# Paged attention over a cache: key steps in pairs, transposes shared by two engines, scores by full-depth runs of 128 keys

## The reference

```python
def latent_scores(q_lat, q_pe, c, k_pe):
    s = jnp.einsum('bqhc,bkc->bhqk', q_lat, c) + jnp.einsum('bqhr,bkr->bhqk', q_pe, k_pe)
    return s.astype(jnp.float32) * MLA_SCALE

def sample_attention(q_lat, q_pe, c_new, kpe_new, c_past, kpe_past):
    s_past = latent_scores(q_lat, q_pe, c_past, kpe_past)
    ...
    p = jax.nn.softmax(jnp.concatenate([s_past, s_new], axis=-1), axis=-1).astype(c_new.dtype)
    return jnp.einsum('bhqk,bkc->bqhc', p[..., :P], c_past) + jnp.einsum('bhqk,bkc->bqhc', p[..., P:], c_new)
```

## Time and profile before

| | |
|---|---|
| median of 3 runs | 1033.61 us (1033.48 to 1036.86) |
| the profiled execution's own time | 1032.82 us |
| its span in the trace | 1030.9 us |
| PE busy, DVE busy, ACT busy, POOL busy | 982.4, 506.8, 445.0, 157.9 us |
| the cache attention, first transpose to the last values product | 407.6 to 568.2 us |
| one of its steps, in the middle of the loop | 9.58 us |

### The profile page before, as it was taken

The page is one execution under the profiler, slowest core; times in us unless marked ns, Lnnn a source line. Parts: engine busy times, 40 slices in busy tenths (PEclk is TensorE's granted clock), DMA queues, the critical chain, the costliest instruction groups (busy, mean ns, idle before and its releaser), DMA issues.

```text
span 1030.9 us, 20604 instructions
## 1 busy us (share of the span) xinstructions
PE 982.4 (95%) x8588; PEld 846.4 (82%) x8588; DVE 506.8 (49%) x992; ACT 445.0 (43%) x963; POOL 157.9 (15%) x257
## 2 busy tenths in 40 slices
PE   4999999999989999899999899999999999999997
PEld 4988899877757556566665799999999999999996
DVE  5665867565475485354444532633343234334423
ACT  5545637566646676344444423431232134113312
POOL 1020500255511201344541000000000000000000
PEclk9999969999999999999999899999999999999999
DMA  7312111220024501577772321422222222222302
GB/s 247 122 46 83 43 42 42 62 48 11 2 68 113 208 1 37 195 238 267 237 241 90 109 83 41 144 82 83 87 102 99 82 83 82 83 86 98 105 1 88
DMA packets 31655, 102.58 MB, mean 100 GB/s; under 512 B 14023, under 2 KB 14967, under 8 KB 25218
## 3 DMA queue, kind: packets, MB, share of 16 engines
q1 hardware_dynamic: 22346, 63.50, 18.7%
q0 software_dynamic: 9216, 37.75, 10.7%
HBM read 96.45 MB, written 4.22 MB: 98 GB/s over the span
## 4 chain that ended last, share of the span: by engine, by line
PE 87%; DVE 6%; ACT 3%; issue 2%; DMA 1%; SPq 0%; DVEq 0%; ACTq 0%
PE PS L589 17%; PE PS L591 17%; PE PS L590 17%; PE PS L1078 7%; PE PS L1089 3%; PE PS L1113 3%; PE PS L724 2%; PE PS L1096 2%; PE PS L797 1%; PE PS L828 1%; PE PS L880 1%; PE PS L979 1%; PE PS L571 1%; DMA RAW<-in_w_stream 1%; PE PS L698 1%
## 5 line engine op out<-in xcount | busy, mean ns | idle before, releaser
L589 PE MATMUL PS<-XH,WH 128*128 128x272 f32 (+1 forms) x928 | 271.4, 292 | 1.8 <-DVE WL L1721 1.8
L591 PE MATMUL PS<-XH,WL 128*128 128x272 f32 (+1 forms) x928 | 270.3, 291 | 0.0
L590 PE MATMUL PS<-XL,WH 128*128 128x272 f32 (+1 forms) x928 | 269.5, 290 | 0.0
L589 PEld LDWEIGHTS PS<-XH,WH 128*128 128x128 f32 x928 | 175.9, 190 | 6.8 <-issue 4.2
L590 PEld LDWEIGHTS PS<-XL,WH 128*128 128x128 f32 x928 | 176.2, 190 | 0.0
L591 PEld LDWEIGHTS PS<-XH,WL 128*128 128x128 f32 x928 | 175.9, 190 | 0.0
L1222 ACT ACTIVATE WH<-RAW 128x2048 fp32r<-128x2048 f32 x46 | 88.0, 1913 | 203.1 <-PE PS L591 203.1
L589 PE MATMUL PS<-NH,WH 128*128 128x272 f32 x512 | 149.1, 291 | 0.8 <-DVE WL L1721 0.8
L591 PE MATMUL PS<-NH,WL 128*128 128x272 f32 x512 | 147.6, 288 | 0.0
L590 PE MATMUL PS<-NL,WH 128*128 128x272 f32 x512 | 146.6, 286 | 0.0
L1721 DVE TENSOR_TENSOR WL<-RAW,WH 128x2048 fp32r<-128x2048 f32 (+1 forms) x48 | 108.1, 2252 | 64.6 <-ACT WH L1222 64.2
(11 more groups left out here) (323 smaller groups left out, 1473.0 us busy)
## 6 DMA issues: line engine op xcount, KB each, us to landing
RAW<-in_w_stream SPq DMA_DIRECT2D x47, 1024.0 KB, 4.8
XN<-in_hin SPq DMA_DIRECT2D x4, 512.0 KB, 6.2
out_y_p<-YO SPq DMA_DIRECT2D x4, 512.0 KB, 2.7
CST<-in_big SPq DMA_DIRECT2D x1, 1132.5 KB, 12.8
SS<-in_sstate SPq DMA_DIRECT2D x1, 1024.0 KB, 5.1
out_ssm_s<-SS SPq DMA_DIRECT2D x4, 256.0 KB
CN<-in_cache,IDX POOLq DMA_INDIRECT x64
WQN<-in_wq SPq DMA_DIRECT2D x3, 256.0 KB, 5.8
```

The source lines that it names most:

```text
L589: pe.matmul(PS[:, b, 0:n], wh, xh[:, k, c:c + n], start=(k == 0), stop=False)
L590: pe.matmul(PS[:, b, 0:n], wh, xl[:, k, c:c + n], start=False, stop=False)
L591: last = pe.matmul(PS[:, b, 0:n], wl, xh[:, k, c:c + n], start=False, stop=(k == DT - 1))
```

## The change

The steps are taken in **pairs** `m` (steps `2m` and `2m + 1`).

- The first 128 latent columns of each key are transposed by PE as before (L1084 in the changed kernel), four units to a step, into two PSUM banks in turn (4 and 7), and ACT alone copies them (`cache_copy`, L1685). The copy also sorts the keys, so that the 128 keys of one quarter `q` of the partitions stand in a row.
- The other 128 latent columns and the 32 rotary ones, five blocks of 32, are transposed by DVE in blocks of 32x32 from `CN` to `CB` (`block_transpose`, L2213, one for each sequence and step, 640 numbers on each partition). Nothing goes through PSUM there, and POOL's packing is gone.
- Scores stand in PSUM banks 0 to 3, one bank for each quarter of the partitions, 256 keys of a pair in each. `column_scores(n)` makes 16 matmuls of 128 keys over 128 rows. `block_scores(m)` makes 80 matmuls of 256 keys, each on 32 rows and 32 columns of the array (`QS` holds the queries laid out anew for that, filled by 32 small DMAs on SP's queue ahead of the loop).
- One maximum over 1024 scores on each row, one correction and one accumulation to a pair; two exponentials, two transposes of P (banks 5 and 0), two copies, two values products.
- `gather(n)` still waits for `ce_pv` of step `n - 4`; an odd one waits for `column_scores(n - 2)` as well.

```diff
-    cn_at = [[x + rows_of * b for b in range(4)] for x in (w_at, w_at + 4 * rows_of, x_at + 4 * rows_of, r1)]
+    cn_at = [[x + rows_of * b for b in range(4)] for x in (w_at, w_at + 4 * rows_of, x_at + DT * T * 4, r1)]
...
+            sp.wait_ge(sem("dve_step"), DVE_STEP["q_padded"])
+            for q in range(4):
+                rows = slice(32 * q, 32 * q + 32)
+                for s in range(4):
+                    src = slice(32 * s, 32 * s + 32)
+                    sp.dma_start(QS[rows, :, s, :], QF[src, :, 1, :]).then_inc(sem("wkbt_in"), 16)
+                    sp.dma_start(QS[rows, :, 4, src], QRF[src, :, src]).then_inc(sem("wkbt_in"), 16)
...
+            def block_scores(m):
+
+                pe.wait_ge(sem("cb_done"), 8 * m + 8)
+                for x in range(5):
+                    for q in range(4):
+                        rows = slice(32 * q, 32 * q + 32)
+                        for b in range(4):
+                            heads = slice(32 * b, 32 * b + 32)
+                            last = pe.matmul(PS[heads, q, 0:2 * P], QS[rows, m // 4, x, heads],
+                                             CB[b][rows, x, :, :, :].rearrange("p s j k -> p (s j k)"),
+                                             start=False, stop=(x == 4))
                 last.then_inc(sem("ct_used"), 1)
...
+            def column_scores(n):
+
+                s = n % 2
+                pe.wait_ge(sem("ct_copied"), 4 * n + 4)
+                if s == 0 and n >= 2:
+                    pe.wait_ge(sem("ce_exp"), n)
+                    pe.wait_ge(sem("ce_ptc"), n)
+                for q in range(4):
+                    for b in range(4):
+                        heads = slice(32 * b, 32 * b + 32)
+                        last = pe.matmul(PS[heads, q, P * s:P * s + P], QF[:, n // 8, 0, heads],
+                                         CT[s][b][:, q, :, :].rearrange("p j k -> p (j k)"),
+                                         start=(s == 0), stop=False)
+                last.then_inc(sem("ct_used"), 1)
...
+            step_transposes(0)
+            step_transposes(1)
+            column_scores(0)
+            for m in range(8):
+                column_scores(2 * m + 1)
+                block_scores(m)
+                if m < 7:
+                    step_transposes(2 * m + 2)
+                cache_p(2 * m)
+                cache_p(2 * m + 1)
+                for x in range(8):
+                    cache_values(2 * m + x // 4, x % 4)
+                if m < 7:
+                    column_scores(2 * m + 2)
+                    step_transposes(2 * m + 3)
...
+            for x in range(8):
+                cache_copy(x // 4, x % 4)
+            for m in range(8):
+                if m < 7:
+                    cache_copy(2 * m + 2, 0)
+                    cache_copy(2 * m + 2, 1)
+                cache_exp(m)
+                cache_copy_p(2 * m)
+                correction(m)
+                cache_copy_p(2 * m + 1)
+                if m < 7:
+                    cache_copy(2 * m + 2, 2)
+                    cache_copy(2 * m + 2, 3)
+                    for b in range(4):
+                        cache_copy(2 * m + 3, b)
...
+            def block_transpose(n, b):
+                if b == 0:
+                    dve.wait_ge(sem(f"cn_in{n % 4}"), 64 * (n // 4 + 1))
+                    if n >= 2:
+                        dve.wait_ge(sem("ct_used"), 3 * (n // 2 - 1) + 3)
+                dve.transpose(CB[b][:, :, n % 2, :, :].rearrange("p x j k -> p j x k"),
+                              CN[n % 4][b][:, :, P:].rearrange("p j (x c) -> p j x c", c=32)).then_inc(sem("cb_done"), 1)
...
+            for x in range(8):
+                block_transpose(x // 4, x % 4)
+            for m in range(8):
+                cache_max(m)
+                if m < 7:
+                    for x in range(8):
+                        block_transpose(2 * m + 2 + x // 4, x % 4)
+                accumulate(m)
...
-            for n in range(2, 16):
-                if n >= 3 and n + 1 < 16:
-                    pool.wait_ge(sem("ce_pv"), n - 2)
-                    gather(n + 1)
-                pack_rope(n)
+            for n in range(4, 16):
+                pool.wait_ge(sem("ce_pv"), n - 3)
+                if n % 2:
+                    pool.wait_ge(sem("ct_used"), 3 * (n // 2 - 1) + 2)
+                gather(n)
```

More of the change, by code:

```diff
@@ L1075, in cache_transposes @@
                     pe.wait_ge(sem(f"cn_in{n % 4}"), 64 * (n // 4 + 1))
                 for j in range(4):
-                    src = CN[n % 4][u % 4][:, j, P * (u // 4):P * (u // 4) + P] if u < 8 else KRN[n % 2][:, j, :, :]
-                    last = pe.transpose(PS[:, CT_BANKS[x % 4], P * j:P * j + P], src, ident)
+                    last = pe.transpose(PS[:, 4 + 3 * (x % 2), P * j:P * j + P], CN[n % 4][b][:, j, 0:P], ident)
                 last.then_inc(sem("ct_mm"), 1)
-            def cache_scores(n, c):
-                if c == 0 and n >= 2:
-                    pe.wait_ge(sem("ce_exp"), n - 1)
-                g, bank = n // 8, 3 + n % 2
-                for b in range(4):
-                    wait_copied(pe, n, 4 * c + b)
-                for b in range(4):
-                    last = pe.matmul(PS[32 * b:32 * b + 32, bank, :], QF[:, g, c, 32 * b:32 * b + 32], CT[4 * c + b][:, :],
-                                     start=(c == 0), stop=False)
-                last.then_inc(sem("ct_used"), 1)
@@ L1117, in _, with cache_values @@
-            for n in range(18):
-                for u in range(9):
-                    if n < 16:
-                        cache_transposes(n, u)
-                    if 1 <= n <= 16 and u == 1:
-                        cache_scores(n - 1, 1)
-                        cache_rope_scores(n - 1)
-                    if n >= 2 and u == 3:
-                        cache_values(n - 2)
-                    if n < 16 and u == 5:
-                        cache_scores(n, 0)
-                    if 1 <= n <= 16 and u == 8:
-                        cache_p(n - 1)
+            def cache_values(n, j):
+                s = n % 2
+                if j == 0:
+                    pe.wait_ge(sem("ce_ptc"), n + 1)
+                    if s == 0 and n >= 2:
+                        pe.wait_ge(sem("acc_done"), n // 2)
+                for b in range(4):
+                    last = pe.matmul(PS[32 * b:32 * b + 32, 6, 0:KV], PTE[:, 4 * s + j, 32 * b:32 * b + 32],
+                                     CN[n % 4][b][:, j, 0:KV], start=(s == 0 and j == 0), stop=(s == 1 and j == 3))
+                if j == 3:
+                    last.then_inc(sem("ce_pv"), 1)
```

189 lines of the change are left out of this document (82 added, 107 removed).

## The result

The changed kernel takes **1081.33 us** (median of 4 runs, 1077.98 to 1083.93) against 1033.78 for the kernel before (4 runs): a ratio of 1.0453, interval 1.0431 to 1.0475. It is slower by 4.5%, where 1009 us and a gain were forecast. The profiled execution took 1083.93 us, 1082.1 of it in the trace.

The account below looks back on a forecast made before the run. PE was taken to bound the kernel (busy 95%), then the gathers at 16.6 us a pair: 27.7 us less, 3 back for the clock, so 24.7 off 1032.8 gives 1008.1, plus 0.8 for the median: 1009 us, range 995 to 1036.

Parts of the forecast that it names:

- the sum: Whole kernel: start to 418.0, six cycles of 16.6 us, then 23.0; 27.7 us less, 24.7 after a clock allowance.
- Rival 5: Loop: engines stand still while DMA engines are full; a 3.7 us stop every second pair gives 1024 us; chance 0.10.
- the 3 us that I had put aside for the clock: Allowance in the total for PE's clock falling once or twice in the loop: 3 us.
- Rival 2: Loop: PE's clock falls to its lower level in every pair, some 3 us a pair, giving 1027 us; chance 0.14.
- forecast 15.3: Loop: the cycle of a pair that the engines alone give, without waiting for gathers, 15.3 us.
- The cycle of 16.6 that the gathers set: Loop: the even gather's keys land at x+16.5, so a pair takes 16.6 us and PE waits 1.3 (bounds 15.8 and 17.3).
- rival 3: Loop: DVE's block transposes are slow, 3.3 us each instead of 0.86, giving a cycle of 30 and 1105 us; chance 0.08.
- block_scores, 2.2 forecast: PE in each pair: 160 passes of 256 keys in ten turns, all 16 tiles at once, 2.2 us.
- rival 4: block_scores on PE: row groups follow one another, 8.6 us, giving 1052 us; chance 0.09 for the full case.
- The test I gave: Changed trace: the forecast is wrong if PE waits for `cb_done` or block_scores shows 4 us or more.

Follow-up runs that it names:

- Run 12: Changed kernel, but from step 4 on each of the four indirect DMAs of a step fetches 64 bytes per partition instead of 4608: 1082.72 us, ratio 1.0462.
- run 5: Changed kernel with the gathers of steps 4 to 15 replaced by plain DMAs of the same bytes from SP's queue, same waits: 1016.41 us.
- run 1: Changed kernel with the gathers of steps 4 to 15 left out (old keys used again): 1011.36 us.
- run 9: Changed kernel with the keys of steps 4 to 15 fetched by plain DMAs from POOL's own queue, same waits and bytes: 1016.08 us.
- run 2: Changed kernel with 64 of the 80 matmuls of block_scores left out: 1008.82 us.
- run 7: Changed kernel with only one of the four indirect DMAs of each step from 4 on, other keys old: 1019.34 us.
- run 3: Changed kernel without the odd gather's wait for column_scores: 1021.46 us.
- run 17: Changed kernel with the odd step's four indirect DMAs issued at separate points, the even step's four still in a row: 1024.72 us, ratio 0.9959.
- run 15: Changed kernel with the odd gather waiting for the end of block_scores instead of column_scores: 1043.7 us, ratio 1.0106.

## Why the prediction was wrong

**The step that failed** is the sum's price for PE's work beside a gather. It counts `block_scores`, the transposes and the column scores at the pace that they have alone, and lets a gather cost PE something only when it lands. Rival 5, "engines stand still while the DMA engines are full", had the matter, with the wrong cause and too low a price. The fact behind it was read rightly: DVE's stop of 3.70 us with its input done is the hold. But I laid it to the DMA share of 1.01 and to eight gathers in a row, and gave it one stop in every second pair, 4 x 3.7. Run 12 has the hold at a share of 0.03, and run 5 has none at 0.78; it comes with the issues of every gather, so twice in a pair.

What it measured, for a pair of 27.0 us against 15.8 in run 1, from stage start to stage start: block_scores 9.8 for 3.3 (+6.5); the odd step's transposes 5.4 for 3.2 and the column scores ahead of them 1.9 for 1.0 (+3.1); the even step's transposes and the odd step's column scores, at the lower clock, 3.2 for 2.5 and 1.9 for 1.0 (+1.6). That is 11.2. From the first to the last even step's transposes, 426.97 to 591.44, six pairs take 164.5 us where six of 16.6 were forecast: 64.9 more. The start has 9.0 more (427.0 for 418.0). Of these run 1 has 4.7 too, on a chip without the hold: `block_scores` begins at half clock there and takes 6.9 us for 2.2. The rest is the hold of the first column scores (6.4 us for 1.95). The end has 3.9 more. With the 3 us that I had put aside for the clock this gives 74.8 of the 75.8 between 1083.9 and 1008.1.

**Rival 2, the clock:** right in kind, too small alone. It falls in every pair, after PE has got its passes in fives and sixes. Of the 11.2 us the lower clock is 1.6 as above, about 1.7 in the last 79 passes of block_scores (3.33 us at half clock, an estimate: half at full), and up to 0.9 in its first 53 (2.0 us, where the pace of run 1 gives 1.1), some 4 in all; I had said 3. It is a consequence: without the hold it stays full in the pairs shown of runs 1, 5 and 9.

**Right:** where PE isn't held, its cycle is nearly as laid out: 15.8 us (forecast 15.3), in run 1 and in some pairs of runs 5 and 9. The cycle of 16.6 that the gathers set shows in run 2, where they do bind, at 17.3. A gather of the changed kernel takes 9.6 to 10.6 us from issue to last byte (10.2), the even one starts 2.23 us behind the values product (2.24). A block transpose is 0.81 us (0.86), so rival 3 falls, and the maximum 1.23 (1.2).

**Luck:** the 16.7 us of runs 5, 7 and 9 look like the forecast's 16.6 and aren't. No DMA stands in the chain of these pairs; a stop inside `block_scores` makes them longer than 15.8. In the changed kernel the keys are never waited for in the chain either, since PE comes later than they do.

**Without the hold,** 1009 us isn't shown either. The changed kernel itself never ran on such a chip. The nearest there are run 3 (1021.46, beside 1027.32) and run 17 (1024.72, beside 1028.87): gains of 0.6 and 0.4%, where the forecast had 2.4%. Both have the gathers placed otherwise, so how much of the rest is the change's own stays open.

**block_scores, 2.2 forecast:** 3.3 undisturbed, ten turns of 0.33 and not of 0.215. Row groups do overlap, so rival 4 falls: one after another they would take 8.6. In the last pair the first 14 passes start 6 to 7 ns apart, later ones mostly 16 to 17. That all sixteen tiles run at once isn't shown. The Trainium skill (TensorE: Matmul & The Clock Gate, section "Wait — 56ns, not 53.3ns?") has no starts closer than about 25 ns; the trace disagrees.

**The test I gave:** I wrote that the forecast falls if `block_scores` shows 4 us or more. It showed 9.9, and by that test I would have taken rival 4; only the last pair (3.9) and the runs in which PE isn't held tell the two apart.

## What to carry to other kernels

When a profile shows an engine's input done and the engine idle ("remote", or a releaser that ended long before), find out what was being issued just then, on every queue, before the kernel is made to depend on that hand-over. Slack of three interleaved steps hid a delay of 2 us in each; the tighter cycle of pairs paid it twice. And a remedy seen in one run on one chip is a finding about that chip until it has been run beside the unmended kernel.

## What the runs showed of the hardware

- While POOL issues indirect DMAs (0.94 us each, 1.25 apart), PE gets five or six passes in 0.73 us where its work is dense: for 1.2 us with one (run 7), for 5.0 with four. With four in a row PE's semaphore updates leave up to 2.7 us late (3.4 in run 15); with eight, up to 8.3; with one at a time, 0.05 at most. Plain DMAs from the same queue (0.52 us each) don't do it, and the bytes don't matter. DVE's and ACT's own updates left on time in the same stretch (0.01 us).
- Through what PE and POOL meet stays open. A hold of matmuls alone could be late instructions, but the late updates of matmuls that the trace gives as done don't fit that. The instruction queue shows nothing either: its packets take 0.93 to 1.41 us in the two pairs shown and 0.90 to 1.40 in run 9, and none moves between 471 and 482 us. Every timed execution carries the profiler's records, so whether these have a part in it is open too; it wasn't tried.
- On some chips it isn't there. Single stops of PE at "issue" are another thing: they stand inside block_scores in runs without indirect DMAs too (0.40 us in run 1, 0.87 in run 5, 1.28 in run 9), and on the chips without the hold up to 3.98 us (run 3). What makes them stays open.
- The same kernel before took 1027 to 1029 us on the chips without the hold, and 1034 to 1035 on the others.
